# The down projection of a decoder layer's MLP in seven block products for eight

## What is computed

```python
def ffn_sublayer(x, g_pre, w_up_l, w_down_l, g_post):
    h = rmsnorm(x, g_pre)
    a = jax.nn.relu(jnp.einsum('btd,df->btf', h, w_up_l))
    return x + rmsnorm(jnp.einsum('btf,fd->btd', a * a, w_down_l), g_post)
```

## Time and profile before

| | |
|---|---|
| median of 3 runs | 2623.96 us (2621.02 to 2625.25) |
| the profiled execution's time | only its span is recorded: 2616.5 us |
| PE busy | 2570.5 us, 98% |
| POOL, ACT, DVE busy | 1296.8, 934.8, 761.8 us |
| granted TensorE clock, mean | 0.996 |
| DMA | 373.72 MB, mean 143 GB/s |

### The profile page before, as it was taken

The page is one execution under the profiler, slowest core; times in us unless marked ns, Lnnn a source line. Parts: engine busy times, 40 slices in busy tenths (PEclk is TensorE's granted clock), DMA queues, the critical chain, the costliest instruction groups (busy, mean ns, idle before and its releaser), DMA issues.

```text
span 2616.5 us, 34806 instructions
## 1 busy us (share of the span) xinstructions
PE 2570.5 (98%) x13946; PEld 2226.2 (85%) x13946; DVE 761.8 (29%) x1667; ACT 934.8 (36%) x1594; POOL 1296.8 (50%) x832
## 2 busy tenths in 40 slices
PE   7999999999999999999999999999999999999998
PEld 6899999999996467788888888878888878898997
DVE  6431111266663225311112111232111234112114
ACT  4001110087775534432234223253323244332232
POOL 1210000067762565855556567476567365654553
PEclk9999999999999999999999999999999999999999
DMA  5312314289977954543345354355454253532332
GB/s 185 113 41 67 109 59 121 69 174 191 172 141 205 297 172 153 193 145 129 113 145 194 129 173 145 112 178 176 149 175 145 98 178 126 171 130 92 131 129 89
DMA packets 264105, 373.72 MB, mean 143 GB/s; under 512 B 78677, under 2 KB 199069, under 8 KB 259033
## 3 DMA queue, kind: packets, MB, share of 16 engines
q1 hardware_dynamic: 243410, 263.37, 35.4%
q10 hardware_dynamic: 14518, 89.43, 9.5%
q0 software_dynamic: 6016, 18.68, 2.5%
HBM read 323.39 MB, written 103.76 MB: 163 GB/s over the span
## 4 chain that ended last, share of the span: by engine, by line
PE 91%; POOL 2%; DVE 2%; ACT 1%; issue 1%; DMA 1%; SPq 0%; ACTq 0%; DVEq 0%; POOLq 0%
PE ml_y L1911 31%; PE ml_up L1869 8%; PE ml_up L1871 8%; PE ml_up L1870 8%; PE pj_acc L481 6%; PE pj_acc L483 6%; PE pj_acc L482 6%; PE at_o L1150 5%; PE at_turn L1130 3%; PE at_score L1119 2%; PE at_score L1120 1%; PE de_s L2574 1%; POOL ml_w_lo L1784 1%; PE de_kt L2555 1%; PE ml_y L1906 1%
## 5 line engine op out<-in xcount | busy, mean ns | idle before, releaser
L1784 POOL TENSOR_TENSOR ml_w_lo<-em_raw,ml_w_hi 128x1024 fp32r<-128x1024 f32 x288 | 700.9, 2435 | 449.3 <-ACT ml_w_hi L1956 449.3
L1956 ACT CAST ml_w_hi<-em_raw 128x1024 fp32r<-128x1024 f32 x288 | 301.7, 1048 | 546.5 <-PE ml_y L1911 353.0
L1911 PE MATMUL ml_y<-ml_w_hi,ml_a_hi 128*128 128x512 f32 x1216 | 475.9, 391 | 3.3 <-POOL ml_w_lo L1784 3.3
L1911 PE MATMUL ml_y<-ml_w_hi,ml_a_lo 128*128 128x512 f32 x1216 | 473.4, 389 | 0.0
L1911 PE MATMUL ml_y<-ml_w_lo,ml_a_hi 128*128 128x512 f32 x1216 | 473.4, 389 | 0.0
L1869 PE MATMUL ml_up<-ml_h_hi,ml_w_hi 128*128 128x512 f32 (+1 forms) x1280 | 450.0, 352 | 1.9 <-POOL ml_w_lo L1784 1.9
L1871 PE MATMUL ml_up<-ml_h_hi,ml_w_lo 128*128 128x512 f32 (+1 forms) x1280 | 449.7, 351 | 0.0
L1870 PE MATMUL ml_up<-ml_h_lo,ml_w_hi 128*128 128x512 f32 (+1 forms) x1280 | 449.6, 351 | 0.0
L481 PE MATMUL pj_acc<-pj_h_hi,pj_w_hi 128*128 128x424 f32 (+1 forms) x800 | 290.0, 363 | 5.8 <-DVE pj_h_lo L699 5.8
L482 PE MATMUL pj_acc<-pj_h_lo,pj_w_hi 128*128 128x424 f32 (+1 forms) x800 | 283.2, 354 | 0.0
L483 PE MATMUL pj_acc<-pj_h_hi,pj_w_lo 128*128 128x424 f32 (+1 forms) x800 | 283.2, 354 | 0.0
(11 more groups left out here) (274 smaller groups left out, 3342.4 us busy)
## 6 DMA issues: line engine op xcount, KB each, us to landing
em_raw<-in_w_up SPq DMA_DIRECT2D x64, 1024.0 KB, 5.3
em_raw<-in_w_down SPq DMA_DIRECT2D x64, 1024.0 KB, 5.1
out_o_a_k_s<-in_cache_a_k ACTq DMA_DIRECT2D x8, 3060.0 KB, 12.6
out_o_a_v_s<-in_cache_a_v ACTq DMA_DIRECT2D x8, 3060.0 KB, 12.1
em_raw<-scratch_pt SPq DMA_DIRECT2D x34, 512.0 KB, 7.0
em_raw<-in_w_out SPq DMA_DIRECT2D x16, 1024.0 KB, 5.0
scratch_pt<-pj_proj SPq DMA_DIRECT2D x10, 1056.0 KB, 4.1
pj_w<-in_w_in SPq DMA_DIRECT2D x20, 512.0 KB, 3.9
```

The source lines that it names most:

```text
L1784: nc.gpsimd.tensor_tensor(split_of(w_lo, n), raw_of(n), f32(split_of(w_hi, n)), ALU.subtract).then_inc(w_lo_ready, 1)
L1911: last = pe.matmul(out, p[:, f, t0:t0 + m], w[:, b, :], start=(f == 0 and p is act_hi and w is hi), stop=(f == PF - 1 and p is act_lo))
L1956: nc.scalar.copy(split_of(w_hi, n), raw_of(n)).then_inc(w_hi_ready, 1)
```

## The change

The down projection is computed by the seven products of the Strassen-Winograd scheme on 2 x 2 blocks: two halves of a group's 512 prompt rows (tiles 0, 1 and tiles 2, 3), two blocks of 256 FF rows, two halves of D. A part is now 512 FF rows (`PARTS` = 8): 4 up units and 7 down units, one per product, each with 2 tiles x 2 FF blocks x 3 = 12 matmuls. The order is P1, P7, P2, P6, P5, P3, P4. The hidden values of both halves are laid out in slots. DVE forms four sums of activations (`first_sums`, `second_sums`, L2403, 128x512) and four of weights (`w_sum`, L2447, 128x1024, in place in `raw`). ACT splits seven operands' high parts; POOL the low parts of P1, P7, P6, P3, P4 (L1916), DVE those of P2 and P5 (L2425). POOL splits ten of eleven weights (L1911), DVE that of P3 (L2451). Each product has its own bank per tile; P2, P3 and P4 accumulate onto the bank of P1, P5 and P7 after DVE has added that one (`ONTO`, L2479). P1 and P6 go into `shared`, which four operations add to the result once per group (L2500, L2504). The samples are computed by ordinary products in four of the seven units. `y` of a group now stays in its `mixed` buffer. Norm work hangs on the slots `SLOTS`. The last norm's gains go from DVE to POOL (`gain_first`, `gain_second`), and `close` orders DVE's last sums.

```diff
-    PARTS = 4
+    PARTS = 8
...
+    P1, P7, P2, P6, P5, P3, P4 = range(7)
+    PRODUCTS = 7
+    ONTO = {P2: P1, P3: P5, P4: P7}
...
+    LO_BY_DVE = (P3,)
...
+    BANK, BEFORE = {}, {}
+    latest, held = {b: -1 for b in range(Y_BANKS)}, {}
+    for step in UNITS:
+        kind, g, part, i = step
+        for j in sums_of(step):
+            q = sum_at(step, j)
+            if kind == "down" and i in ONTO and j < PAIRS:
+                bank = held.pop((g, part, ONTO[i], j))
+            else:
+                bank = min((b for b in latest if b not in held.values()), key=lambda b: latest[b])
+                if kind == "down" and i in ONTO.values() and j < PAIRS:
+                    held[g, part, i, j] = bank
+            BANK[q], BEFORE[q] = bank, latest[bank]
+            latest[bank] = q
+
+    LOADS = []
...
+    SLOTS = (("up", 0, 0), ("up", 0, 2), ("down", 0, P1), ("down", 0, P5), ("up", 1, 0), ("up", 1, 2), ("up", 1, 3))
...
+        def wait_load_spent(engine, load):
+
+            kind, g, part, i = LOADS[load]
+            if kind != "down":
+                wait_lo(engine, UNIT_OF[kind, g, part, i + 1])
+            else:
+                for product in ((P6, P4), (P5, P3))[i]:
+                    wait_lo(engine, UNIT_OF["down", g, part, product])
...
+            def load_raw(load):
+                kind, g, part, i = LOADS[load]
+                wait_load_spent(sp, load - RAW)
...
             def split_lo(n):
+                if n >= NU or lo_by_dve(n):
+                    return
                 pool.wait_ge(w_hi_ready, n + 1)
                 nc.gpsimd.tensor_tensor(split_of(w_lo, n), raw_of(n), f32(split_of(w_hi, n)),
                                         ALU.subtract).then_inc(w_lo_ready, 1)
...
+            def low(at, his, slot, frm):
+                pool.wait_ge(a_hi_done, 7 * at + his)
+                nc.gpsimd.tensor_tensor(a_lo[:, slot, :], frm, f32(a_hi[:, slot, 0:2 * HT]), ALU.subtract).then_inc(a_lo_done, 1)
...
-                if n + AHEAD < NU:
-                    split_lo(n + AHEAD)
-                if step[0] == "up":
-                    low(step)
+                kind, g, part, i = step
+                at = part_of(step)
+                split_lo(n + AHEAD)
+                if kind == "up" and i == DF:
+                    low(at, 1, SLOT[P1], a[:, 0, :, :].rearrange("p f t -> p (f t)"))
+                    low(at, 2, SLOT[P7], a_raw[:, SLOT[P7], :])
...
+                if kind == "down" and i == P1:
...
+                    pool.wait_ge(a_summed, 4 * at + 4)
+                    low(at, 4, SLOT[P6], a_raw[:, SLOT[P6], :])
+                if kind == "down" and i == P2:
+                    low(at, 6, SLOT[P3], a_raw[:, SLOT[P3], :])
+                    low(at, 7, SLOT[P4], a_raw[:, SLOT[P4], :])
...
+            def product_down(n):
...
+                wait_lo(pe, n)
+                wait_operand(step)
...
+                for j in sums_of(step):
+                    q = sum_at(step, j)
+                    pe.wait_ge(y_added, BEFORE[q] + 1)
...
+                    out = y_ps[BANK[q]][:, :]
+                    for f in range(DF):
+                        c = f * HT + j * P
+                        for p, w in ((a_hi, hi), (a_hi, lo), (a_lo, hi)):
+                            last = pe.matmul(out, p[:, SLOT[i], c:c + P], w[:, f, :],
+                                             start=(i not in ONTO and f == 0 and p is a_hi and w is hi),
+                                             stop=(f == DF - 1 and p is a_lo), skip_group_check=i in ONTO)
                     last.then_inc(y_done, 1)
...
-                act.wait_ge(raw_in[n // 2 % RAW], 16 * (n // 2 // RAW + 1))
...
+                if kind == "down" and i in (P7, P6, P5, P4):
+                    act.wait_ge(w_summed, 4 * part_of(step) + (P7, P6, P5, P4).index(i) + 1)
+                else:
+                    wait_loaded(act, load_of(step))
                 if n >= SPLIT:
                     wait_used(act, n - SPLIT)
                 nc.scalar.copy(split_of(w_hi, n), raw_of(n)).then_inc(w_hi_ready, 1)
...
+                    split_hi(n + AHEAD)
...
+                        if i == DF:
+                            act.wait_ge(y_done, FIRST_Q[step])
+                            act.wait_ge(emptied, turns_through(("up", g, part, DF - 1)))
+                            high(SLOT[P1], a[:, 0, :, :].rearrange("p f t -> p (f t)"))
...
+                            act.wait_ge(a_summed, 4 * at + 1)
+                            high(SLOT[P7], a_raw[:, SLOT[P7], :])
...
+                        relu(step)
+                    if kind == "down" and i == P1:
+                        act.wait_ge(emptied, turns_through(("up", g, part, PF - 1)))
+                        high(SLOT[P2], kept_raw)
...
+                        act.wait_ge(a_summed, 4 * at + 3)
+                        high(SLOT[P6], a_raw[:, SLOT[P6], :])
+                    if kind == "down" and i == P7:
+                        high(SLOT[P5], a_raw[:, SLOT[P5], :])
+                        act.wait_ge(a_summed, 4 * at + 4)
+                        high(SLOT[P3], a_raw[:, SLOT[P3], :])
+                    if kind == "down" and i == P2:
+                        high(SLOT[P4], a_raw[:, SLOT[P4], :])
...
             def hidden(step):
                 kind, g, part, i = step
...
+                    at = hidden_of(step, c)
+                    dve.wait_ge(relu_done, relus_before(step) + c + 1)
+                    last = nc.vector.scalar_tensor_tensor(at, src[:, 0:at.shape[1] * HT].rearrange("p (q t) -> p q t", t=HT), 0.0, at,
+                                                          ALU.max, ALU.mult)
...
+            def a_sum(to, one, other, op):
+                nc.vector.tensor_tensor(to, one, other, op).then_inc(a_summed, 1)
...
+            def first_sums(step):
+                dve.wait_ge(emptied, turns_through(step))
+                a_sum(a_raw[:, SLOT[P7], :].rearrange("p (f t) -> p f t", t=HT), a[:, 0, :, :], a[:, 1, :, :], ALU.subtract)
+
+            def second_sums(step):
+                kind, g, part, i = step
+                at = part_of(step)
+                by_f = [a_raw[:, s, :].rearrange("p (f t) -> p f t", t=HT) for s in range(DBLK)]
+                dve.wait_ge(emptied, turns_through(step))
+                a_sum(by_f[SLOT[P5]], a[:, 1, :, :], by_f[SLOT[P4]], ALU.add)
+                dve.wait_ge(a_summed, 4 * at + 2)
+                a_sum(by_f[SLOT[P6]], by_f[SLOT[P5]], a[:, 0, :, :], ALU.subtract)
+                dve.wait_ge(a_summed, 4 * at + 3)
+                a_sum(by_f[SLOT[P3]], by_f[KEPT], by_f[SLOT[P6]], ALU.subtract)
...
+            def low(at, his, slot, frm):
+                dve.wait_ge(a_hi_done, 7 * at + his)
+                nc.vector.tensor_tensor(a_lo[:, slot, :], frm, f32(a_hi[:, slot, 0:2 * HT]), ALU.subtract).then_inc(a_lo_by_dve, 1)
...
+                    wait_lo(dve, UNIT_OF["down", g, part, P1])
+                    dve.wait_ge(w_summed, 4 * part_of(step) + 1)
+                    to, one, other, op = left[:, top], right[:, top], left[:, top], ALU.add
+                if which == P5:
+                    wait_lo(dve, UNIT_OF["down", g, part, P7])
+                    dve.wait_ge(w_summed, 4 * part_of(step) + 2)
+                    to, one, other, op = right[:, top], right[:, bottom], left[:, top], ALU.subtract
+                if which == P4:
+                    wait_lo(dve, UNIT_OF["down", g, part, P2])
+                    to, one, other, op = left[:, bottom], left[:, bottom], left[:, top], ALU.subtract
+                nc.vector.tensor_tensor(to, one, other, op).then_inc(w_summed, 1)
+
+            def split_lo(n):
+                dve.wait_ge(w_hi_ready, n + 1)
+                nc.vector.tensor_tensor(split_of(w_lo, n), raw_of(n), f32(split_of(w_hi, n)), ALU.subtract).then_inc(w_lo_by_dve, 1)
...
+            def add_down(step, j):
+                kind, g, part, i = step
+                q = sum_at(step, j)
+                src, at = y_ps[BANK[q]][:, :], mixed(g)
+                left, right = slice(0, HALF), slice(HALF, D)
+                dve.wait_ge(y_done, q + 1)
...
+                elif i in (P1, P6):
+                    add_sum(shared[:, j, :], src, part == 0 and i == P1)
+                elif i in (P7, P5):
+                    add_sum(at[:, PAIRS + j, right], src, part == 0 and i == P7)
+                elif i == P4:
+                    add_sum(at[:, PAIRS + j, left], src, part == 0)
+                else:
+                    add_sum(at[:, j, left if i == P2 else right], src, part == 0)
...
                     if kind == "up":
+                        if g and part == 0 and i == 0:
+                            share(g - 1)
+                        if i == DF:
+                            w_sum(step, P7)
+                        if i == PF - 1:
+                            w_sum(step, P6)
+                            w_sum(step, P5)
                         hidden(step)
```

(16 more changed lines are left out.)

609 lines of the change are left out of this document (388 added, 221 removed).

## The result

| | before | changed kernel |
|---|---|---|
| median | 2624.61 us (2621.02 to 2627.58, 4 runs) | 2835.83 us (2825.99 to 2840.68, 4 runs) |
| profiled span | 2616.5 us | 2833.1 us |
| ratio | | 1.0797, 95% interval 1.0774 to 1.0821 |

It is 211 us slower, 8%. The forecast was 2784 (2680 to 2865). Four of them (the short splits, the norms from a bank, the second change of the tail, and all together) ran on another chip than the rest, with the kernel before beside them but not the changed kernel.

The account below looks back on a forecast made before the run. TensorE, busy 98% of 2616.5 us, was taken to bound the kernel. 2616.5 - 87 (matmuls) + 255 (stalls) - 8 (tail) = 2776.5, with 7.5 from span to median 2784 us; range 2680 to 2865.

Parts of the forecast that it names:

- Fewer matmuls, -87.0: Down projection: 7 blocks of 12 matmuls for 8, 384 fewer over 32 parts, worth -87.0 us.
- Exclusion of DVE's two-SBUF operations and POOL for a whole instruction: DVE operations in SBUF meeting POOL wait up to 2.4 us plus 1.07 (0.54 for 512); POOL pays those 1.07.
- Rival 1: No exclusion between DVE and POOL operations: plain parts 40.80 us, only norm parts stall, 2598 us in all; chance 0.12.
- the narrow one: Skill's VectorE Performance Modes read alone: only two-port instructions block POOL, so fp32 sums of two tensors cost nothing.
- Plain parts, 6.14 of stall: Parts without norms: PE stalls 6.14 us each, 46.9 for an ideal 40.8; 67 us for 11 parts.
- The first wait: At P2, needing the addition of P1.0 delayed on DVE: it starts at 7.52, not 5.44, a stall of 2.08 us.
- the step that failed: At P6.1, waiting for P2.0's bank behind DVE's queue: it starts at 14.90, not 11.82, a stall of 3.08 us.
- The walk: Step-by-step timing of a plain part: stalls of 2.08, 3.08 and 0.76 us; 3.8 if DVE alone pays.
- Rival 4: PE's stalls lower its clock: judged no effect except on norm parts, inside the range; no chance given.
- Norm parts, 53 to 55 us by shared holding: Six parts with residual additions and norms: DVE and POOL holding gives 53 to 55 us; stalls of 91 in all.
- Last group, 3.4 us over its cover in each other part: Other parts of the last group: 6.4 us more PE work as cover, leaving 3.4 x 6 = 20 us.
- Tail, -8: Behind the last matmul: one sum comes with the last product and POOL takes the gains, -8 us (0 to -12).

Follow-up runs that it names:

- the short splits: Changed kernel, POOL subtracting only the first half of each 128 columns run in the seven products' weight splits: ratio 1.0098, 2647.9 us.
- the norms from a bank: Changed kernel with DVE sums, low parts and norms of groups 0 to 2 reading one operand from PSUM: ratio 1.0253, 2688.9 us.
- the second change of the tail: Changed kernel, POOL's first-half gain multiplications waiting for the samples' sums and the second halves' given to DVE: ratio 1.0788, 2828.9 us.
- all together: Changed kernel with spread norms, the tail edits, all eleven weight splits on POOL, and these halved in group 3: ratio 1.0770, 2825.1 us.
- the run with PSUM operands: Changed kernel with DVE's sums and low parts in groups 0 to 2 taking one operand from PSUM: ratio 1.0332, 2706.4 us.
- the run with later gains: Changed kernel with POOL's five first-half gain multiplications waiting for the samples' sums: ratio 1.0809, tail 24.4 us.
- The filled wait: Changed kernel with 8 extra matmuls before P2's wait, in all parts but the last of each group: ratio 1.0778, 2822.8 us.

## Why the prediction was right, and where not

The direction, the size (+160 forecast, +211 measured) and the first mechanism stand. That the size comes so near is in part luck, as the sum behind the steps shows. By its steps:

1. *Fewer matmuls, -87.0*: right, in number and price.
2. *Exclusion of DVE's two-SBUF operations and POOL for a whole instruction*: right. DVE's weight sums take 2.24 us in the mean (2.3 forecast), POOL's splits 2.59 (2.8 forecast), additions from PSUM 0.69 at most. Moving one operand to PSUM takes it all away in plain parts, to 40.80. Rival 1, no exclusion, is what the run with PSUM operands shows in plain parts, and there alone. The Trainium skill's wider rule ("GPSIMD Engine Reference", Key points: a two-port mode or two SBUF inputs) is the one that this kernel obeys; by the narrow one those operands could have made no difference, and they made 119 us.
3. *Plain parts, 6.14 of stall*: 3.9 to 4.1 measured in group 0 and once 6.4, 5.3 to 8.5 in groups 1 and 2. For the eleven, 62 us over ideal for 67 forecast. The first wait came as forecast (1.97 for 2.08); the step that failed is the one behind it, P6.1. The walk gave the turn to POOL's split and let the low part for P5 wait. In the part shown that low part started within 0.01 us of the split and had the turn, so P6.1 and P5.1 did not wait. Where POOL has it, as in the part of 47.2, they do: 1.32 us for 3.08 and 0.42 for 0.76, and the part lasts about the 46.9 of the forecast. The slow clock was in neither: it takes the place of 1.5 us of waiting. In the fifth part of group 0 of the run with later gains POOL has the turn and no matmul is at 0.427: there P6.1 waits 2.82, near the 3.08, and the part lasts 47.2 all the same.
4. *Rival 4, "no effect" of stalls on the clock*: wrong. It was read from a window in which PE was busy 91 of 100 us at clock 1.00, but that says nothing of one gap of 2 us. Here waits of 2 us and more bring matmuls at 0.427, though not each time, 54 us in all in those of 512 columns. The filled wait shows that in groups 0 to 2 this costs little of its own: it lies where PE would wait for POOL. Stalls and clock together were 277 us (186.5 + 90.2), for 255 forecast.
5. *Norm parts, 53 to 55 us by shared holding*: the size is low (60.2 to 63.3) and the mechanism wrong. Without exclusion they keep 53 to 56. What stays without it, 14 us per part over ideal in the mean, is the larger piece, and exclusion adds 6 to 9. In the one slot that was followed it is the queues of ACT, DVE and POOL in order; for the others that is inferred. The forecast's own sum was loose here too: 53 to 55 is 12 to 14 over 40.8, which gives 73 to 85 us for six parts and not 91.
6. *Last group, 3.4 us over its cover in each other part*: measured 54.6, 6.4 over an ideal of 48.2. The forecast had 6.4 us more of PE work and an ideal of 47.2; the kernel before takes 101.8 us for 1024 FF rows of this group, so 50.9 for 512, and less 2.72 that is 48.2, 7.4 more. This work lies in the up steps and sample products, while the waits are at P2: the samples' product there waits up to 3.2 us for its bank (20.2 us in seven parts by the waits of PE), which the forecast did not name.
7. *Tail, -8*: wrong in sign, +16.4. I had read DVE's work from 2596 to 2611 as lying behind the last matmul, which ended at 2608.6. And the ten multiplications given to POOL cost 1.25 each where DVE takes 0.68; giving five back won 2.7 us, so most of the tail has another cause, not shown.

So the forecast was 24 us too low in the tail and 22 in stalls and clock: 2776.5 + 24 + 22 is 2823, and the late start of that execution makes most of the rest to 2833. The 22 are what is left of larger errors of both signs: the six norm parts have 119 us over ideal for 91, the other parts of the last group 37 for 20, the plain parts 62 for 67, and all others together, by subtraction, about 60 for 76.

## What to carry to other kernels

Add up the work of DVE and POOL as one engine wherever DVE reads two SBUF tensors, and look for the moment at which each meets the other: both were under 60% busy here and still cost 120 us. An engine works in order, and what stands at its head delays all behind it (PE waited 7.06 us for a split queued behind a residual addition), so look for a place for a small task (a norm, a residual) where no weight split queues behind it; spreading the norms, tried here, won 8 us at most. Before a wait is moved, ask what the bounding engine does meanwhile: taking PE's 2 us away let POOL idle and cost 105.

## What the runs showed of the hardware

- TensorE's granted clock fell to its half level for 7 matmuls, 1.5 us after a wait of 1.97 us had ended; with 1.81 us of that wait filled it stayed at 1.00. It also stayed at 1.00 behind a wait of 2.10 us in the part before.
- Of a DVE and a POOL operation that start within 0.02 us of each other either can have the turn: DVE in 13 of 20 parts, POOL in 7, and the parts differ by 2.3 us.
- A DVE operation on two SBUF tensors can lose its turn many times: 6.58 us for one of 0.68, until five POOL operations back to back had ended. With POOL operations half as long, the longest weight sum fell from 3.45 to 2.42 us.
- With one input in PSUM the same operations were never stretched: 1215 ns for 2352 in the mean (128x1024), 682 for 1348 (128x512).
